# A weight split moved to GpSimd, and copies put in another order on ScalarE and VectorE, in a two-layer fp32 transformer kernel

## The reference

```
h = h + mixed @ w_out                      # mixed: three kinds of attention heads, concatenated
f = rms_norm(h, ffn_norm)
gate, up = split(f @ w_gate_up)            # two times 2816 columns
h = h + (silu(gate) * up) @ w_down
```

## Time and profile before

| | us |
|---|---|
| median of 3 runs | 1273.78 (1273.47 to 1273.92) |
| the profiled execution | 1273.78 |
| its span | 1271.8 |
| PE busy | 1252.4 |
| DVE, ACT, POOL busy | 926.8, 661.2, 289.5 |
| HBM read and written | 108.79 MB and 2.10 MB |

### The profile page before, as it was taken

The page is one execution under the profiler, slowest core; times in us unless marked ns, Lnnn a source line. Parts: engine busy times, 40 slices in busy tenths (PEclk is TensorE's granted clock), DMA queues, the critical chain, the costliest instruction groups (busy, mean ns, idle before and its releaser), DMA issues.

```text
span 1271.8 us, 23210 instructions
## 1 busy us (share of the span) xinstructions
PE 1252.4 (98%) x9174; PEld 1184.5 (93%) x9174; DVE 926.8 (73%) x1540; ACT 661.2 (52%) x1100; POOL 289.5 (23%) x168
## 2 busy tenths in 40 slices
PE   7999999999999999999999999999999999999998
PEld 7989999999999999999998889988899999998886
DVE  4598889578999999822236999984889999986100
ACT  5575547655555555622234756386655555554221
POOL 2554313100000000144446462221000000003443
PEclk9999999999999999999999999999999999999999
DMA  5222200132332221233323221100322322213333
GB/s 192 89 64 84 67 34 34 34 116 83 118 115 100 100 100 68 101 100 99 99 83 98 73 84 66 52 35 18 132 99 101 133 101 100 100 67 100 111 104 115
DMA packets 27442, 113.60 MB, mean 89 GB/s; under 512 B 3664, under 2 KB 4304, under 8 KB 21968
## 3 DMA queue, kind: packets, MB, share of 16 engines
q1 hardware_dynamic: 26624, 111.18, 25.3%
q10 hardware_dynamic: 720, 1.09, 0.2%
HBM read 108.79 MB, written 2.10 MB: 87 GB/s over the span
## 4 chain that ended last, share of the span: by engine, by line
PE 89%; DVE 6%; issue 2%; ACT 1%; POOL 1%; DMA 0%; SPq 0%; DVEq 0%; POOLq 0%; ACTq 0%
PE ps L1254 22%; PE ps L868 20%; PE ps L1260 11%; PE ps L874 10%; PE ps L965 5%; PE ps L971 5%; PE ps L966 5%; PE ps L1095 2%; PE ps L1068 1%; PE ps L1078 1%; PE ps L1043 1%; DVE score L1911 1%; PE ps L1152 1%; PE ps L931 1%; PE ps L1110 1%
## 5 line engine op out<-in xcount | busy, mean ns | idle before, releaser
L748 POOL TENSOR_TENSOR wlo<-raw,whi 128x1024 fp32r<-128x1024 f32 x96 | 236.0, 2460 | 917.6 <-ACT whi L1353 637.3
L1353 ACT ACTIVATE whi<-raw 128x1024 fp32r<-128x1024 f32 x116 | 122.6, 1057 | 217.2 <-PE ps L874 174.3
L965 PE MATMUL ps<-xhi,whi 128*128 128x264 f32 (+1 forms) x632 | 177.6, 310 | 0.0
L966 PE MATMUL ps<-xlo,whi 128*128 128x264 f32 (+1 forms) x632 | 171.4, 300 | 0.0
L868 PE MATMUL ps<-hhi,whi 128*128 128x264 f32 (+1 forms) x528 | 157.5, 321 | 0.2 <-DVE hlo L2187 0.2
L868 PE MATMUL ps<-hlo,whi 128*128 128x264 f32 (+1 forms) x528 | 157.6, 321 | 0.0
L965 PEld LDWEIGHTS ps<-xhi,whi 128*128 128x128 f32 x632 | 119.1, 189 | 4.5 <-issue 0.4
L966 PEld LDWEIGHTS ps<-xlo,whi 128*128 128x128 f32 x632 | 119.2, 189 | 3.9
L868 PEld LDWEIGHTS ps<-hhi,whi 128*128 128x128 f32 x528 | 99.4, 188 | 8.1 <-DVE hlo L2187 0.4
L868 PEld LDWEIGHTS ps<-hlo,whi 128*128 128x128 f32 x528 | 99.1, 188 | 7.8
L971 PE MATMUL ps<-xhi,wlo 128*128 128x264 f32 (+1 forms) x632 | 102.4, 304 | 0.0
(11 more groups left out here) (277 smaller groups left out, 3281.5 us busy)
## 6 DMA issues: line engine op xcount, KB each, us to landing
raw<-in_weights SPq DMA_DIRECT2D x116, 512.0 KB, 3.2
raw<-in_groups SPq DMA_DIRECT2D x42, 1024.0 KB, 4.8
out_hT<-h SPq DMA_DIRECT2D x7, 256.0 KB, 4.3
h<-in_hT SPq DMA_DIRECT2D x4, 264.0 KB, 6.2
h<-in_hT ACTq DMA_DIRECT2D x4, 264.0 KB, 5.7
cst<-in_consts SPq DMA_DIRECT2D x1, 780.5 KB, 9.1
xnb<-feat SPq DMA_DIRECT2D x20, 33.2 KB, 2.0
feat<-xnb SPq DMA_DIRECT2D x20, 33.2 KB, 2.0
```

Source lines behind the costliest of these rows:

```text
L748: nc.gpsimd.tensor_tensor(wlo[:, b], raw[:, b], whi[:, b].bitcast(F32), ALU.subtract).then_inc(split_done, 1)
L965: nc.tensor.matmul(o, whi[:, k % 2, n], xhi[:, n, cut], start=(n == 0), stop=False)
L966: nc.tensor.matmul(o, whi[:, k % 2, n], xlo[:, n, cut], start=False, stop=False)
L1353: return nc.scalar.activation(whi[:, b], raw[:, b], ACT.Copy).then_inc(hi_done, 1)
```

## The change

1. *Last split of the output projection.* DVE's split of `U_GU` goes from m = 7 (ahead of `xlo` of m = 7) to the end of m = 6.
2. *ACT in the output projection.* `forms_high` of an even m goes from ahead of `round_unit` to behind the square. In m = 7 `round_unit` of `U_GU+1` goes from ahead of `xhi` to behind it.
3. *ACT in the groups.* `q0` waits for `gate_scaled` of the group before instead of its `x_sum` (whose semaphore goes away; DVE waits for its own step instead), and silu comes between `q0` and `q1` instead of behind `q1`.
4. *Down projection.* The splits of `U_DN` and `U_DN+1` go from DVE to POOL, and POOL's wait for them goes away.

The amount of arithmetic and the number of DMAs stay as they were.

```diff
 # POOL
-                pool.wait_ge(split_done, l * UNITS + (U_DN + 4))
-                for n in range(U_DN + 2, UNITS + (2 if l < DEPTH - 1 else 0)):
+                for n in range(U_DN, UNITS + (2 if l < DEPTH - 1 else 0)):
                     split_unit(l * UNITS + n, n % 2)
 # ACT, output projection
                 for m in range(KT):
-                    if m and m % 2 == 0:
-                        forms_high(m // 2 - 1)
-                    round_unit(U_OUT + m + 2, m % 2)
+                    if m < KT - 1:
+                        round_unit(U_OUT + m + 2, m % 2)
                     act.wait_ge(ev.acc_free, 2 + m + 1)
                     x_high(m, par[:, P_FFN + m:P_FFN + m + 1], of)
+                    if m == KT - 1:
+                        round_unit(U_OUT + m + 2, m % 2)
...
                                              scale=par[:, P_FFN + m:P_FFN + m + 1]).then_inc(sv.odd_scaled, 1)
+                    elif m:
+                        forms_high(m // 2 - 1)
 # ACT, groups
                     if n > 1:
-                        act.wait_ge(sv.x_summed, g0 + n - 1)
+                        act.wait_ge(sv.gate_scaled, l * MF + n)
                     snapshot(n, "a22_b22", "y", s0[:, 0:width])
+                    silu_gate(n - 1)
                     if n > 2:
                         act.wait_ge(sv.hidden, l * MF + n - 1)
                     snapshot(n, "f1_v", "z", s1[:, n % 2, 0:width])
-                    silu_gate(n - 1)
 # DVE, output projection
-                    if m == KT - 1:
-                        split_unit(U_GU, 0)
...
-                    if m % 2 == 0 and m < KT - 2:
+                    if m % 2 == 0:
                         split_unit(U_OUT + m + 2, 0)
-                    elif m % 2 and m < KT - 1:
+                    elif m < KT - 1:
                         forms_begin(m // 2)
                         forms_end(m // 2)
 # DVE, groups
-                    nc.vector.tensor_tensor(x, x, s0[:, 0:width], ALU.add).then_inc(sv.x_summed, 1)
-                    dve.wait_ge(sv.x_summed, g0 + n)
+                    chain(nc.vector.tensor_tensor(x, x, s0[:, 0:width], ALU.add))
 # DVE, down projection
-                split_unit(U_DN, 0)
                 gate_join(GROUPS_7)
...
                     hidden_low(k)
-                    if k == EARLY_HID + 4:
-                        split_unit(U_DN + 1, 1)
```

More of the change, by code:

```diff
@@ L394, in __init__ @@
         self.sg_ready = sem("sg_ready")
-        self.x_summed = sem("x_summed")
         self.hhi_ready = sem("hhi_ready")
```

## The result

The changed kernel takes 1283.29 us at the median (1282.46 to 1284.03), the kernel before 1273.73 beside it: a ratio of 1.0073, with a 95% interval of 1.0061 to 1.0085. It is slower by 9.6 us, where 4.3 was forecast, and 1.8 us beyond the upper end of the range (1281.5). The profiled execution took 1282.98 us with a span of 1281.1 us, 9.3 more than the span before.

What follows compares the result with a forecast made beforehand. PE, busy 98% of the span, was taken as the bound. Layer 0 (+0.15 +1.0 -0.3 -0.4 = +0.45) and layer 1 (+2.6 +1.65 -0.4 = +3.85) gave +4.3 on 1273.78: 1278.1 us, range 1275.0 to 1281.5 (8 in 10).

Steps and rivals of the forecast that it cites:

- four of its places of loss: PE waits for `whi` of `U_GU+1` (0.15 layer 0, 2.6 layer 1) and `q0` of group 2 (1.0, 1.65 us).
- The pair time of DVE: Output projection: a pair of units takes DVE 11.3 us instead of 9.96, against PE's 11.1 in layer 1.
- The `whi` of `U_GU+1`: End of output projection: PE waits for this rounding, 0.15 us in layer 0 and 2.6 in layer 1.
- `q0` in group 2, with `lo_raw_b`: Group 2: PE waits for `q0` 1.0 and 1.65 us (layers 0, 1), saves 0.3 and 0.4 on `lo_raw_b`.
- the first rival: Down projection: POOL's second split goes ahead of `hlo` of tile 7 in both layers; +7.1, 1280.9 us, chance 0.25.
- The collision at tile 7: Down projection: POOL's `U_DN+1` split against `hlo`; cost taken as 0, upper bounds 2.15 (layer 0) and 0.65 us (layer 1).
- The rule of the Trainium skill that the text used: Down projection: POOL and DVE contend where DVE reads two SBUF inputs; `gate_join` goes on, only `hlo` is caught, 2.91 us.

Runs made afterwards that it cites:

- experiments 4 and 6: 4: changed kernel with `round_unit` of `U_GU+1` back ahead of `xhi` in m = 7, 1280.36 us; 6: kernel before with parts 3 and 4 only, 1278.13 us.
- experiment 11: Changed kernel in which POOL waits for the `hlo` of tile 7 before it splits `U_DN+1`: 1278.71 us, ratio 1.0043.
- experiment 3: Kernel before with part 4 only, the splits of `U_DN` and `U_DN+1` on POOL: 1273.14 us, ratio 0.9998.

## Why the prediction was wrong

Its direction and all four of its places of loss were right; the size was not, by 5.3 us at the median (9.6 against 4.3). By its steps:

- **The pair time of DVE.** Forecast: 2.99 from add to `flo`, 11.3 a pair, the add of m = 7 at 928.4. Measured: 2.95, 11.21, and 931.24, which is 928.2 after taking off the 3.08 by which layer 1 started late. Right. The low weights and the loads that queue behind them came in time, as said.
- **The `whi` of `U_GU+1`.** Forecast 2.6 and, in layer 0, 0.15; measured 2.56 and 0.29. Right. The times at which PE wants it were taken from the chain of waits, 0.16 later than the timeline has them, which makes up the 0.14 of layer 0; in layer 1 the rounding also ended about 0.2 sooner than forecast, and the two cancel. The claim that with the rounding ahead of `xhi` the add would be waited for by 0.9 was measured as 0.79.
- **`q0` in group 2, with `lo_raw_b`.** Forecast 1.0 - 0.3 and 1.65 - 0.4; measured 1.19 - 0.23 and 1.60 - 0.46. Right within 0.3.
- **What the stall of 2.6 us does to PE itself** was not in the sum. Its price was taken as its length. In the profiled run the clock was at 0.50 for the eight multiplications behind it: +1.60. The runs with longer and shorter stalls show that this belongs to the stall. No rival had it either: the first rival's +7.1 and this 1.6 make 8.7.
- **The collision at tile 7, "lower bound 0, the value I take".** This is the step that failed. Forecast: no wait of PE, in either layer. Measured: 2.04 and 0.63, together 2.7 more, and just under the upper bounds given (2.15 and 0.65). The text placed the two "within 0.1 of each other", which is about what came (0.19), and then took the end that costs nothing without a reason for that order. The runs show that the 0.5 us by which part 3 moves POOL decides: part 4 alone costs nothing, with part 3 it costs 2.8, with POOL held it costs nothing again. The rule of the Trainium skill that the text used (GPSIMD Engine Reference, Key points) holds in these rows: beside POOL's first split, `up` and `x_sum`, which have an input in PSUM, take their usual 0.42 and 0.43 us, and the `hlo`, with both inputs in SBUF, is held by the second.
- **The last 0.5 us** of the 9.3 are spread over places of 0.2 and less and not traced.

The miss is thus two terms: 2.7 for the collision and, in the profiled run, 1.6 for the clock. Without the collision the time would have fallen inside the range. The rival "POOL takes the port first" (1280.9, chance 0.25) had the right set of places.

What stays open: how often the clock falls. The 31 runs of the changed kernel lie in three groups: 6 at 1280.84 to 1281.70, near the sum without the fall (1282.98 - 1.6 = 1281.4), 17 at 1282.46 to 1283.37, and 8 at 1283.90 to 1284.28, these with a mean clock of 0.997 where all others have 0.999. With the same stall of 2.5 us and no collision, 2 of 8, 2 of 4 and 1 or 2 of 4 runs were slower by such a step. The collision is itself a stall of 2.0 us, and experiments 4 and 6, in which it is the longest stall that the change adds, have such slower runs too (2 of 4, 1 of 4). So the clock may fall behind either stall, and behind both in the slowest group. This is not shown: every profile has the clock at 1.00 around tile 7. Taking the collision away gives back 4.1 us (9.6 less 5.5) where its own waits are 2.3 more than before, so the other 1.8 us of the difference between medians may be of this kind.

## What to carry to other kernels

Moving work off the critical engine's neighbours is safe only as long as both orders of arrival are safe: where two engines reach something that they share within some tenths of a us, take the costly end for the forecast, or write the order down, as the one wait in experiment 11 does. Price a stall of PE like the ones here, 2.5 us and longer, at more than its length, since the multiplications behind it may run at half clock. And a lateness that one stall hides is still there when the stall is removed, so parts must be tried together as well as alone.

## What the runs showed of the hardware

- A POOL split holds up a DVE instruction with both inputs in SBUF: an `hlo` of 0.71 us lasts 2.74 to 2.90 if it is issued just behind the start of a split. Between two splits that stand back to back on POOL, a waiting `hlo` got in (0.93 us, experiment 3); one that was issued 0.19 after the second had begun did not.
- The granted clock fell from 1.00 to 0.50 behind stalls of PE of 2.5 us and more, in stages that are otherwise at 1.00, for seven or eight multiplications of 512 columns, in a share of the runs that grew with the stall (0 of 11 at 1.6 us, 5 of 5 at 5.3, by time and mean clock). The same kernel pays it in one run and not in the next. The Trainium skill (TensorE: Matmul & The Clock Gate, Part 1) says the like of a kernel's start, where it calls the number of slow multiplications run-variable; that number was not compared between runs here.
- The view's clock does not show every slow stretch: the first multiplications of 264 columns in the kernel before, from 6.99 us on, follow each other at 0.22 us instead of 0.122 until about 12 us, half the pace, after PE had waited 6.6 us for its first weights, while the windows there have 1.00. No run tells the cause.
- A stall for a semaphore can stand in the profile as "issue" (the 2.40 us above): the instruction on ACT that ended 0.1 before PE went on tells the cause, and the stall grew to 5.33 us with eight copies put ahead of that instruction.
